# Down-projection weights of a mixture-of-experts loop fetched as one 16 KB run per partition, with the inner units renumbered to match

## What is computed

```python
def expert_block(a):
    xb, e = a
    gate, up = jnp.split(xb @ w_gate_up[e], 2, axis=-1)    # (1024, 2*512)
    return (jax.nn.silu(gate) * up) @ w_down[e]            # (512, 1024)
```

## Time and profile before

| what | us |
|---|---|
| median of 3 runs | 2142.19 |
| lowest and highest run | 2139.87, 2154.58 |
| the profiled execution | 2152.84 |
| its span, first to last instruction | 2150.9 |
| PE busy in the span (matmul) | 1699.6 (79%) |
| DVE, ACT, POOL busy | 487.9, 324.3, 121.9 |
| L883, gate and up matmuls, busy | 474.6 |
| L896, down matmuls, busy | 263.1 |
| L928, gate and up of further passes, busy | 53.5 |

### The profile page before, as it was taken

One profiled execution on the slowest core, in us unless ns is written; L12 is line 12 of the kernel. 1 busy time (PEld: TensorE's weight loads), 2 busy tenths in 40 slices (PEclk: granted clock), 3 DMA queues, 4 the chain that ended last, 5 costly groups with the idle time before them and its releaser, 6 DMA issues.

```text
span 2150.9 us, 25298 instructions
## 1 busy us (share of the span) xinstructions
PE 1699.6 (79%) x8325; PEld 783.4 (36%) x8326; DVE 487.9 (23%) x1022; ACT 324.3 (15%) x601; POOL 121.9 (6%) x147
## 2 busy tenths in 40 slices
PE   5988687687947888787887679989748788788682
PEld 3433233345432433333332334434523333233231
DVE  1679344320150101000000132120410000000003
ACT  3022334222020000001110220000200011010001
POOL 0012000120120000000000100001010000000001
PEclk9999888798967999999999879999679999899996
DMA  9951586685047596999999930201468899999995
GB/s 353 416 172 70 204 306 235 228 301 227 0 161 311 214 414 259 401 419 417 423 423 420 350 139 0 79 0 41 195 243 329 324 416 422 421 423 422 421 423 214
DMA packets 144964, 604.27 MB, mean 281 GB/s; under 512 B 15952, under 2 KB 18289, under 8 KB 128362
## 3 DMA queue, kind: packets, MB, share of 16 engines
q1 hardware_dynamic: 113648, 522.55, 61.1%
q10 hardware_dynamic: 21025, 46.17, 5.7%
q0 software_dynamic: 10208, 34.48, 4.5%
HBM read 551.57 MB, written 52.01 MB: 281 GB/s over the span
## 4 chain that ended last, share of the span: by engine, by line
PE 63%; DMA 12%; DVE 10%; issue 7%; ACT 4%; POOL 1%; SPq 1%; ACTq 1%; DVEq 0%; POOLq 0%
PE ps L883 19%; PE ps L896 10%; PE ps L1008 8%; DMA ring<-in_w_gate_up_dram 5%; PE ps L578 5%; PE ps L594 3%; DMA ring<-in_w_down_dram 2%; PE ps L928 2%; PE ps L623 2%; PE ps L906 1%; DVE W L1483 1%; PE ps L940 1%; PE ps L520 1%; PE ps L496 1%; PE ps L718 1%
## 5 line engine op out<-in xcount | busy, mean ns | idle before, releaser
L883 PE MATMUL ps<-ring,W 128*64 128x512 f32 x2048 | 474.6, 615 | 48.3 <-issue 33.2
L896 PE MATMUL ps<-ring,W 128*64 128x512 f32 x1024 | 263.1, 659 | 54.7 <-DVE W L1806 49.3
L883 PEld LDWEIGHTS ps<-ring,W 128*64 128x64 f32 x2048 | 175.8, 141 | 335.1 <-issue 335.1
L1033 ACT ACTIVATE W<-ps 128x512 f32<-128x512 f32 (+3 forms) x244 | 138.1, 579 | 899.1 <-PE ps L896 353.8
L1800 DVE TENSOR_TENSOR W<-W,ps 128x256 f32<-128x256 f32 x64 | 27.0, 422 | 788.9 <-ACT W L1334 788.9
L1008 PE MATMUL ps<-hT,ring 128*128 128x512 f32 x384 | 168.0, 597 | 0.0
L896 PEld LDWEIGHTS ps<-ring,W 128*64 128x64 f32 x1024 | 88.0, 151 | 188.3 <-issue 188.2
L1008 PEld LDWEIGHTS ps<-hT,ring 128*128 128x128 f32 x384 | 72.8, 191 | 94.5 <-issue 94.5
L623 PE MATMUL ps<-ring,hT 128*128 128x512 f32 x192 | 88.6, 618 | 1.9 <-DVE W L1498 1.9
L1334 ACT ACTIVATE W<-ps 128x256 f32<-128x256 f32 x64 | 24.6, 384 | 423.3 <-PE ps L883 423.1
L1483 DVE SCALAR_TENSOR_TENSOR W<-W,prm 128x512 f32<-128x512 f32 x116 | 85.3, 805 | 0.0
(11 more groups left out here) (305 smaller groups left out, 1396.7 us busy)
## 6 DMA issues: line engine op xcount, KB each, us to landing
ring<-in_w_gate_up_dram SPq DMA_DIRECT2D x128, 2048.0 KB, 15.8
ring<-in_w_down_dram SPq DMA_DIRECT2D x64, 2048.0 KB, 15.0
ring<-in_w_ada_dram SPq DMA_DIRECT2D x24, 2048.0 KB, 9.1
x_rows<-X ACTq DMA_DIRECT2D x1, 18944.0 KB, 71.5
ring<-in_cache_k_dram SPq DMA_DIRECT2D x64, 256.0 KB, 3.2
W<-x_rows SPq DMA_DIRECT2D x32, 512.0 KB, 15.4
x_rows<-W ACTq DMA_DIRECT2D x128, 128.0 KB, 6.7
ring<-in_cache_v_dram POOLq DMA_DIRECT2D x48, 256.0 KB, 5.1
```

Source lines behind the costliest of these rows:

```text
L883: x = mm(ps[CAP * z:CAP * z + CAP, 2 + j, :], xt[:, k, :], at[:, :, 256 * z:256 * z + 256], start=(k == 0), stop=(k == KD - 1))
L896: x = mm(ps[CAP * z:CAP * z + CAP, 5 + j, :], ht[:, k % 2, CAP * (k // 2):CAP * (k // 2) + CAP], ring[:, 3 * j + 2, at:at + 512], start=(k ...
L1033: return fn(out, src, ACT.Copy, **k)
```

## The change

Partition p of a down slot now holds weight rows 4p to 4p + 3, one run of 16 KB in HBM. So chunk k of the down product holds units 4p + k, and the columns of gate and up are taken to match: tile z of `gate_up` reads the units 4f + 2z and 4f + 2z + 1 for f from 0 to 127, that is two neighbouring elements out of every four (8 of every 16 bytes), and `h_turns` takes every second column of the product. In a further pass tile z reads every fourth column of gate and of up. The counts of instructions, their shapes, PSUM tiles, semaphores and the order of issue stay. The transfer's size stays; its number of runs in HBM falls from 512 to 128.

```diff
             def experts(l):
                 gu = a["w_gate_up"][l].rearrange("e (p k) n -> e p k n", p=P)
-                dn = a["w_down"][l].rearrange("e (k p) n -> e p k n", p=P)
+                dn = a["w_down"][l].rearrange("e (p k) n -> e p k n", p=P)
...
                 def gate_up(xt, j, half, signal):
                     for k in range(4 * half, 4 * half + 4):
-                        at = ring[:, 3 * j + half, D * (k % 4):D * (k % 4) + D].rearrange("p (g f) -> p g f", g=2)
+                        at = ring[:, 3 * j + half, D * (k % 4):D * (k % 4) + D].rearrange("p (g f r) -> p g f r", g=2, r=4)
                         for z in range(2):
-                            x = mm(ps[CAP * z:CAP * z + CAP, 2 + j, :], xt[:, k, :], at[:, :, 256 * z:256 * z + 256],
+                            x = mm(ps[CAP * z:CAP * z + CAP, 2 + j, :], xt[:, k, :], at[:, :, :, 2 * z:2 * z + 2],
                                    start=(k == 0), stop=(k == KD - 1))
...
                 def h_turns(src, j, signal):
                     for k in range(2):
-                        x = tr(ps[:, 4 + 3 * j, P * k:P * k + P], src[:, P * k:P * k + P], ident)
+                        x = tr(ps[:, 4 + 3 * j, P * k:P * k + P], src[:, k:2 * P:2], ident)
...
-                                at = ring[:, 3 * j + half, D * (k % 4):D * (k % 4) + D].rearrange("p (g f) -> p g f", g=2)
+                                at = ring[:, 3 * j + half, D * (k % 4):D * (k % 4) + D].rearrange("p (g f r) -> p g f r", g=2, r=4)
                                 for z in range(4):
-                                    x = mm(ps[XC * z:XC * z + XC, 2 + j, 0:256], xT2[:, k, :], at[:, :, P * z:P * z + P],
+                                    x = mm(ps[XC * z:XC * z + XC, 2 + j, 0:256], xT2[:, k, :], at[:, :, :, z],
                                            start=(k == 0), stop=(k == KD - 1))
```

## The result

The changed kernel took 2204.76 us (median of 4 runs, 2196.66 to 2217.09) beside 2143.42 us for the kernel before; the ratio is 1.0278, with a 95% interval of 1.0225 to 1.0332. I had forecast 2132 us in a range up to 2172. It is slower by 61 us, and the direction was that of two of my rivals. The two profiled executions (2152.84 and 2202.95 us) lie 50 us apart, since that of before is one of its longer runs.

The account below looks back on a forecast made before the run. PE sets the pace up to 893 and 1720 us, DMA until 1183 and 2030, then PE. Median 2142.2 less 9.9 us of DMA savings, strided reads at nothing, gives 2132.3 us; own range 2124 to 2142, full range 2122 to 2172.

Parts of the forecast that it names:

- two of my rivals: Further passes slow down (L928 doubles, 2168.9 us, chance 0.15); main matmuls slow down too (L883, about 2560 us, chance 0.10).
- I take nothing for both: Strided moving reads of L883 and L928 were costed at zero, from L906's load; the other end was a doubling.
- a slow reader: Argument against L928 doubling: float32 columns go at about 0.9 ns per column and tile.
- The rule that I set against the row: Skill's 16-byte lines want two hits each for full speed: L883 stays free, L928 pays; set against L906's load.
- the rival that followed from the rule: Further passes slow down: L928 takes 3.66 us more a pass, 36.6 less 9.9, giving 2168.9 us; chance 0.15.
- ten of fourteen passes: Passes where PE sets the pace: seven up to 893 us, three up to 1720; the other four hidden by DMA waits.
- The turns: `h_turns` loads weights at a stride of 2: at most 4 ns, twice an expert, taken as nothing.
- The DMA term: 384 packets fewer per down transfer save 0.27 us; 37 transfers in both layers' full stretches give 9.9 us, range 0 to 11.8.
- my two stretches: Two stretches with DMA full, mixer weights in 2 KB runs and the loop's mix, solved for 11.1 ns per packet.
- The estimate of 3.5 ns: Skill's fixed overhead of about 3 cycles per packet at 850 MHz; the same 37 transfers would save 3.1 us.
- its slack: Layer 1's far end: four experts and a pass want 61 of 76 us, so 5.1 us of DMA savings fit.
- its full stretch: Layer 1, 1720 to 2030 us: DMA never runs dry, so its bytes over the rate set the end.

Follow-up runs that it names:

- down alone: Kernel before with only the down transfer changed, one run of 16 KB per partition in both layers: 2131.99 us, ratio 0.9914, with two passes fewer in layer 1.
- The kernel with both reads contiguous: Changed kernel with gate and up read contiguously in main matmuls and further passes; 16 KB down runs and stride-2 turns remain: 2160.84 us, ratio 1.0047.
- the kernel with down in two runs: Kernel before with down in two 8 KB runs per partition, main matmuls contiguous, turns and passes at stride 2: 2159.32 us, ratio 0.9996.
- half of down: Kernel before, but each layer 1 down transfer moves only two of its four runs per partition (1 MB): 2141.82 us, ratio 0.9917.

## Why the prediction was wrong

**The step that failed** is "I take nothing for both" for the strided moving side of L883 and L928, chosen by the row of a weight load. L928 doubled (3.66 to 7.46 us), L883 paid 4.7% (7.07 to 7.40). The range of that cost had been named rightly, nothing to a doubling, and the value taken from its cheap end because of the wrong neighbour: a load of weights is no guide to the moving side. Even of loads the pair said too little. L906 at a stride of 8 (195 ns) was set against L1008 (191 ns), another line; L906 itself, read contiguously, takes 141 ns for 193, so its stride cost 37% and not 2%. I had also argued against a doubling that float32 columns go at 0.9 ns each, "a slow reader"; one tile alone at a stride of 4 doubles all the same.

**The rule that I set against the row** was right on where the step lies. The Trainium skill (SBUF: State Buffer, section on Door 1) asks for two hits in a line of 16 bytes. The runs agree on that: 612 ns with two hits against 593 contiguous, 1079 and 1098 ns with one, and the same step on two and on four tiles. They do not agree that two hits give full speed: two hits cost 3% on one tile and 5% on two and four, and over 64 experts this is 21 us of PE, twice the gain that I forecast. I gave the rival that followed from the rule 0.15.

**That rival's size** was off too, 2169 for 2205. Its per-pass price was right (3.66 forecast, 3.80 measured). I let only ten of fourteen passes count, since four lay where DMA sets the end, and kept the whole DMA gain. But passes that are longer by 53 us and experts that are longer by 21 give the ring time to fill: waits for weights went from 29.7 to 7.4 us and all fourteen passes counted. In the terms of the loops, the rival had 36.6 - 9.9 = 26.7; the four passes more bring 16.6, the 21.1 of L883, which it had at nothing, are the largest part, the turns bring 4.5, and the waits that went instead of the DMA gain take 12.4 off: 56.5. A cover counted from the old balance goes when the change moves the balance.

**The turns** were costed at 4 ns, from L906 against L1008. No row of before had L889 at a stride; its loads took 140 ns before and 206 after, which is 0.07 us per expert and 4.5 us in all. Small, but half of the gain forecast.

**The DMA term.** The count of packets was right, and so was the full rate: I had written about 425 GB/s, and full windows and slices show 425 to 430. The price per packet was 11.1 ns by my two stretches and 7.7 by a pair that differs in little but run length; that takes the 9.9 us to 6.8. (The first stretch was called one of 2 KB runs; it is one from some 1203 us on only. Taken from 1205 to 1215 us, 1912 packets and 3.88 MB, the same sum gives 9.5 ns.) The estimate of 3.5 ns that stood beside my slope lies below all of these. In layer 1 the gain was there in the profile (7.4 us shorter, waits 8.2 us less). In layer 0 no profile shows it: there waits fell from 10.1 to 5.5 us with down alone, and the loop kept its length, with a granted clock of 0.96 against 0.98 in the window of 893 to 1183 us. The lower clock fits that, and why it was lower was not tested. The prediction had also read the waits for weights as lasting until 1182.85; the bracket there names "issue", and the last one that names a transfer is at 1169.25. And it took some 6 us for a pass where passes of one expert follow each other every 9 us (L918 at 711.95 and 720.90), which its slack bore. No measured time confirms the DMA gain in either layer.

**What stays open.** The kernel with both reads contiguous should have been at 0.999 by these prices (6.8 us gained, 4.5 lost) and was at 1.0047, at least 1.0010. The strided turns alone are not the reason, since the kernel with down in two runs has them too. The lower mean granted clock of the former over ten runs (0.893 for 0.900) goes with the longer time, but what lowered it is not known; that fewer waits for weights are in part paid back by the clock is therefore not excluded, although the kernels with down in one run in layer 1 alone (0.899 for 0.900) and with half of down (0.901 for 0.900) do not show it. Doubling the packets of gate and up cost less than their price, of which the contiguous turns explain up to 7.6 us. These residues are within 10 us, where the runs of one kernel spread over 30.

**Right** were the count of packets and, for layer 1, the reading that DMA sets the end of its full stretch (with all of its 19.6 us of waits gone, its loop was 17.6 us shorter in the profile); for layer 0 no run shows it. The threshold of 5% at which L883's cost alone would cancel the gain was not reached, at 4.7%, and it was too high: it counted 27 experts, while all 64 became longer and the waits that covered the others went.

## What to carry to other kernels

When a layout in memory is bought with a stride on a matmul's moving side, keep two float32 elements in each 16 bytes: then it cost 3 to 5% here, neighbours or not, and otherwise the matmul doubled. Price a strided operand by rows of the same operand and the same line, with and without the stride, and where none exist, let the rule that speaks against the change weigh as much as the bound that it names. A few per cent of DMA rate are worth at most the waits that PE really has for it, here 30 us of 2150; an edit that lengthens PE's own work takes their place, as here, where 22 of the 30 us went and the kernel was still slower.

## What the runs showed of the hardware

- A float32 matmul of 512 moving columns took 593 ns contiguous, 612 at a stride of 2, 1079 at 4 and 1098 at 8, and a group took 14.6 us at a stride of 4 where it takes 7.1, on one tile over the whole array and on two tiles side by side; on four tiles 7.46 us for 3.66.
- What counts fits the number of elements taken from each 16 bytes: two neighbours out of four and every second element cost the same (3.85 us a pass), one out of four doubles (7.46 us), and one out of eight costs only 2% more than one out of four (1098 ns for 1079, on one tile).
- Loading 128 columns of float32 weights at a stride of 2 took 206 ns where contiguous ones took 140 in the same place (L889); at a stride of 8 the medians were 193 ns for 141 contiguous (L906) and 200 for 138 (L918). Contiguous ones at L1008 took 191 on average, so the place matters as much as the stride.
- A DMA packet cost about 7.7 ns beyond its bytes in stretches where DMA was full: 411 GB/s with all weights in 4 KB runs, 421 with a third of them, 425 to 430 with none.
- The same program's runs spread from 2132 to 2171 us over the chips used, with the mean granted TensorE clock between 0.91 and 0.89, which hides a gain of 10 us in single runs.
